# A float32 transformer stack on one core: first slots with input in five pieces, products of ones ahead of it, the first squares on GpSimd and the first mean in the third slot

## The reference

```python
def rmsnorm(x, g):
    xf = x.astype(jnp.float32)
    y = xf * lax.rsqrt(jnp.mean(xf * xf, axis=-1, keepdims=True) + EPS)
    return (y * g.astype(jnp.float32)).astype(x.dtype)

def swiglu(x, w_gate, w_up, w_down):
    return (jax.nn.silu(x @ w_gate) * (x @ w_up)) @ w_down
...
h = h + 0.5 * swiglu(rmsnorm(h, ffn1_norm[l]), ffn1_w_gate[l], ffn1_w_up[l], ffn1_w_down[l])
```

## Time and profile before

| | us |
|---|---|
| median of three runs | 1508.74 (1508.28 to 1511.12) |
| the profiled execution, its own time | 1506.61 |
| its span, first to last instruction | 1504.6 |
| TensorE busy | 1490.0 |
| VectorE busy | 1188.2 |
| ScalarE busy | 795.2 |
| GpSimd busy | 44.5 |

### The profile page before, as it was taken

The page is one execution under the profiler, slowest core; times in us unless marked ns, Lnnn a source line. Parts: engine busy times, 40 slices in busy tenths (PEclk is TensorE's granted clock), DMA queues, the critical chain, the costliest instruction groups (busy, mean ns, idle before and its releaser), DMA issues.

```text
span 1504.6 us, 25373 instructions
## 1 busy us (share of the span) xinstructions
PE 1490.0 (99%) x10802; PEld 1383.0 (92%) x10802; DVE 1188.2 (79%) x1567; ACT 795.2 (53%) x1010; POOL 44.5 (3%) x43
## 2 busy tenths in 40 slices
PE   7999999999999999999999999999999999999999
PEld 6888899999988888888899999999999999999989
DVE  7987777797898865988668678888998899766744
ACT  6444456565554443544446466455535645775653
POOL 0000001210000000000001110000000000000000
PEclk9999999999999999999999999999999999999999
DMA  7555445434555545455544443455554453325531
GB/s 284 200 194 194 172 161 188 150 141 144 191 183 192 196 172 204 184 196 195 183 164 160 180 151 141 159 223 188 200 188 180 158 195 137 117 105 190 184 125 57
DMA packets 38687, 260.50 MB, mean 173 GB/s; under 512 B 4656, under 2 KB 5040, under 8 KB 9136
## 3 DMA queue, kind: packets, MB, share of 16 engines
q1 hardware_dynamic: 37856, 257.84, 47.4%
q10 hardware_dynamic: 720, 1.05, 0.2%
HBM read 257.83 MB, written 1.05 MB: 172 GB/s over the span
## 4 chain that ended last, share of the span: by engine, by line
PE 93%; DVE 5%; ACT 1%; issue 0%; DMA 0%; ACTq 0%
PE ps L260 22%; PE ps L209 14%; PE ps L211 13%; PE ps L210 13%; PE ps L262 11%; PE ps L681 8%; PE ps L683 4%; DVE w_low L199 2%; PE ps L1400 1%; PE ps L1391 0%; PE ps L1380 0%; ACT w_high L192 0%; DMA w_raw<-in_weights 0%; DVE scratch L2072 0%; PE ps L1415 0%
## 5 line engine op out<-in xcount | busy, mean ns | idle before, releaser
L192 ACT ACTIVATE w_high<-w_raw 128x2048 fp32r<-128x2048 f32 (+3 forms) x244 | 458.5, 1880 | 407.8 <-PE ps L211 182.3
L199 DVE TENSOR_TENSOR w_low<-w_raw,w_high 128x2048 fp32r<-128x2048 f32 (+3 forms) x244 | 551.1, 2261 | 116.3 <-ACT w_high L192 114.1
L260 PE MATMUL ps<-x,w_high 128*128 128x512 f32 x1408 | 494.9, 396 | 9.4 <-DVE w_low L811 9.4
L262 PE MATMUL ps<-x,w_low 128*128 128x256 f32 x1408 | 393.6, 280 | 0.0
L260 PEld LDWEIGHTS ps<-x,w_high 128*128 128x128 f32 x1408 | 265.3, 188 | 70.9 <-issue 9.3
L262 PEld LDWEIGHTS ps<-x,w_low 128*128 128x128 f32 x1408 | 266.6, 189 | 0.1
L209 PE MATMUL ps<-x,w_high 128*128 128x256 f32 (+1 forms) x904 | 260.9, 289 | 0.5 <-DVE x L296 0.2
L211 PE MATMUL ps<-x,w_low 128*128 128x256 f32 (+1 forms) x904 | 255.7, 283 | 0.0
L210 PE MATMUL ps<-x,w_high 128*128 128x256 f32 (+1 forms) x904 | 255.6, 283 | 0.0
L681 PE MATMUL ps<-ffn_hid,w_high 128*128 128x512 f32 x528 | 183.2, 390 | 0.0
L209 PEld LDWEIGHTS ps<-x,w_high 128*128 128x128 f32 (+1 forms) x904 | 172.6, 191 | 5.5 <-issue 4.6
(11 more groups left out here) (451 smaller groups left out, 2370.0 us busy)
## 6 DMA issues: line engine op xcount, KB each, us to landing
w_raw<-in_weights SPq DMA_DIRECT2D x229, 1024.0 KB, 4.8
w_raw<-in_weights SPq DMA_DIRECT2D x10, 768.0 KB, 4.2
w_raw<-in_weights SPq DMA_DIRECT2D x5, 512.0 KB, 3.8
even_second_vectors<-in_second SPq DMA_DIRECT2D x1, 1836.0 KB, 8.2
w_raw<-in_weights SPq DMA_DIRECT2D x2, 640.0 KB, 3.9
resid<-in_x SPq DMA_DIRECT2D x4, 256.0 KB, 6.1
w_raw<-in_weights ACTq DMA_DIRECT2D x4, 256.0 KB, 7.6
out<-resid SPq DMA_DIRECT2D x3, 256.0 KB, 2.4
```

What stands on the lines that cost most here:

```text
L192: act.activation(self.wh[:, j, 0:SIZES[n]], self.raw[:, j, 0:SIZES[n]], ACT.Copy).then_inc(self.hi_made, 1)
L199: dve.tensor_tensor(self.wl[:, j, 0:SIZES[n]], self.raw[:, j, 0:SIZES[n]], self.wh[:, j, 0:SIZES[n]].bitcast(F32), ALU.subtract).then_inc( ...
L260: pe.matmul(c.bank(bank + i).rearrange("p (a t) -> p a t", a=2), wh[:, k, f], c.x[:, :, k, :], start=(k == 0), stop=False, skip_group_chec ...
L262: mm = pe.matmul(c.bank(bank + i, SEQ), wl[:, k, f], c.xh[:, k, :], start=False, stop=(k == DT - 1), skip_group_check=True)
```

## The change

- x and slot 0 arrive in five pieces: k tiles 0, 1, 2 to 3, 4 to 5, 6 to 7. The gain vector counts into the first piece's semaphore.
- TensorE issues 18 products of ones (128 x 128) as soon as the ones are there, into a bank that nothing reads.
- GpSimd squares x, two k tiles at a time, as the pieces land, and adds the squares up; ScalarE's four squares and VectorE's four additions of the first norm are gone.
- The first mean is made in the middle of slot 2, no longer in the middle of slot 1.
- In step 0 of the first stage VectorE reads the up result and makes slot 4's low part before the reciprocal, and not behind it; ScalarE makes slot 4's high part before the root.

```diff
-PIECES = 4
+FIRST_TILES = ((0, 1), (1, 2), (2, 4), (4, 6), (6, 8))
+PIECES = len(FIRST_TILES)
+WARM = 18
...
         for s in range(FF_STEPS):
+            late = s == 0 and base == 0
             dve.wait_ge(*self.filled(2 * s + 1))
             take_wide(c, dve, b.gate[:, :, :], B_GATE).then_inc(b.gate_read, 1)
             if s == 0:
                 c.split_low(dve, base + RING)
+            if late:
+                take_up(s)
+                c.split_low(dve, base + 1 + RING)
+            if s == 0:
                 self.norm.reciprocal(dve)
...
-            c.split_low(dve, base + 2 * s + 1 + RING)
+            if not late:
+                c.split_low(dve, base + 2 * s + 1 + RING)
...
-        sp.wait_ge(*self.arrived(1))
+        for b, (first, end) in enumerate(FIRST_TILES):
+            sp.dma_start(c.h[:, first:end, :], self.x[:, first:end, :]).then_inc(self.piece_in[b], 16)
+        sp.wait_ge(*self.arrived(2))
...
+        pool.wait_ge(*self.arrived(0))
+        for b in range(1, PIECES):
+            x = c.h[:, 2 * b - 2:2 * b, :]
+            pool.wait_ge(*self.arrived(b))
+            pool.tensor_tensor(c.sq[:, 2 * b - 2:2 * b, :], x, x, ALU.mult).then_inc(c.sq_made, 1)
+        pool.wait_ge(c.sq_made, PIECES - 1)
+        for i in (0, 4):
+            c.pool_link(pool.tensor_tensor(c.sq[:, i:i + 2, :], c.sq[:, i:i + 2, :], c.sq[:, i + 2:i + 4, :], ALU.add))
+        c.pool_link(pool.tensor_tensor(c.sq[:, 0:2, :], c.sq[:, 0:2, :], c.sq[:, 4:6, :], ALU.add))
+        pool.tensor_tensor(c.sq[:, 0, :], c.sq[:, 0, :], c.sq[:, 1, :], ALU.add).then_inc(c.sum_made, 1)
...
-        for b in range(PIECES):
-            self.norm.square(act, b)
         c.split_high(act, 2)
+
+    def tensor_first(self, pe):
+        c = self.c
+        pe.wait_ge(self.ones_made, 1)
+        for _ in range(WARM):
+            pe.matmul(c.bank(B_DOWN, P), c.ones[:, 0, :], c.ones[:, 1, :], start=True, stop=True)
...
-        self.norm.add(dve)
         c.split_low(dve, 2)
```

More of the change, by code:

```diff
@@ L251, in wide @@
             midway()
-        if norm and k % 2 == 0:
+        if norm and n and k % 2 == 0:
             pe.wait_ge(*norm.x_low(k // 2 + 1))
-        if n == 0 and k % 2 == 0:
-            pe.wait_ge(c.lo_made, k // 2 + 1)
+        for b, (first, _) in enumerate(FIRST_TILES if n == 0 else ()):
+            if k == first:
+                pe.wait_ge(c.xl_made, b + 1)
+                pe.wait_ge(c.lo_made, b + 1)
         if n == 1 and k % 4 == 0:
@@ L664, in tensor @@
                 pe.wait_ge(*self.gate_read(s))
-            wide(c, pe, B_GATE, base + 2 * s, norm=None if s else self.norm).then_inc(c.done, 1)
+            mean = lambda: self.norm.mean(pe)
+            wide(c, pe, B_GATE, base + 2 * s, norm=None if s else self.norm,
+                 midway=mean if s == 1 and base == 0 else None).then_inc(c.done, 1)
             if s:
                 pe.wait_ge(*self.up_read(s))
-            wide(c, pe, B_UP, base + 2 * s + 1, midway=None if s else lambda: self.norm.mean(pe)).then_inc(c.done, 1)
+            wide(c, pe, B_UP, base + 2 * s + 1, midway=mean if s == 0 and base else None).then_inc(c.done, 1)
         for m in range(FF_STEPS):
@@ L751, in __init__, with high, low @@
         self.piece_in = [c.sem(f"piece_in{b}") for b in range(PIECES)]
-        self.gain_in, self.half_in, self.tables_in, self.angle_made, self.sines_made, self.ones_made = (
-            c.sem(s) for s in ("gain_in", "half_in", "tables_in", "angle_made", "sines_made", "ones_made"))
+        self.half_in, self.tables_in, self.angle_made, self.sines_made, self.ones_made = (
+            c.sem(s) for s in ("half_in", "tables_in", "angle_made", "sines_made", "ones_made"))
     def arrived(self, b):
-        return self.piece_in[b], 32
+        return self.piece_in[b], 32 if b else 48
     def piece(self, t, b):
-        return t[:, 0, b * SLOT // PIECES:(b + 1) * SLOT // PIECES]
+        first, end = FIRST_TILES[b]
+        return t[:, 0, first * FC:end * FC]
+    def high(self, act, b):
+        c = self.c
+        act.wait_ge(*self.arrived(b))
+        for k in range(*FIRST_TILES[b]):
+            ins = act.activation(c.xh[:, k, :], c.h[:, k, :], ACT.Copy, scale=self.norm.gain[:, k:k + 1])
+        ins.then_inc(c.xh_made, 1)
+    def low(self, dve, b):
+        c = self.c
+        dve.wait_ge(c.xh_made, b + 1)
+        for k in range(*FIRST_TILES[b]):
+            ins = dve.scalar_tensor_tensor(out=c.xl[:, k, :], in0=c.h[:, k, :], scalar=self.norm.gain[:, k:k + 1],
+                                           in1=c.xh[:, k, :].bitcast(F32), op0=ALU.mult, op1=ALU.subtract)
+        ins.then_inc(c.xl_made, 1)
     def half(self, t, b):
@@ L785, in gpsimd @@
         pool.memset(c.eps[:, :], EPS).then_inc(self.ones_made, 1)
+        pool.wait_ge(*self.arrived(0))
[8 more added lines that the diff above has]
+        pool.tensor_tensor(c.sq[:, 0, :], c.sq[:, 0, :], c.sq[:, 1, :], ALU.add).then_inc(c.sum_made, 1)
     def first_scalar(self, act):
         c = self.c
[L789 to L792, removed]
+        act.dma_start(c.vec[:, 0:DT], self.vectors[:, 0:DT]).then_inc(self.piece_in[0], 16)
+        for b, (first, end) in enumerate(FIRST_TILES):
+            act.dma_start(self.piece(c.raw, b), c.weights[0][:, first * FC:end * FC]).then_inc(self.piece_in[b], 16)
         act.preload_act_table(ACT.Sqrt)
         act.wait_ge(self.ones_made, 1)
-        act.wait_ge(self.gain_in, 16)
         for b in range(PIECES):
-            self.norm.high(act, b)
+            self.high(act, b)
             act.activation(self.piece(c.wh, b), self.piece(c.raw, b), ACT.Copy).then_inc(c.hi_made, 1)
```

27 lines of the change are left out of this document (16 added, 11 removed).

## The result

| | before | changed |
|---|---|---|
| median, us | 1508.91 (1508.28 to 1511.50, 8 runs) | 1513.45 (1511.26 to 1516.82, 8 runs) |
| the profiled execution, its own time | 1506.61 | 1511.26 |
| its span | 1504.6 | 1509.2 |

The ratio is 1.0034, with an interval of 1.0024 to 1.0044: slower by 4.5 us in the medians (0.34% by the ratio), more than the 0.2% that the prediction took as the least a measurement can tell from no change, and just above the upper end of its range (1513.4). The forecast was 1511.3. The direction and the place were right, the size was not.

A forecast was written before the change was run, and what follows sets the result against it. TensorE was busy 1490 of 1504.6 us; slot 4's start was the yardstick. GpSimd's turns put it at 37.7, 2.6 us after 35.09, so 1508.74 + 2.6 = 1511.3 us; the range took in 1506.4 to 1513.4.

The forecast's parts named there:

- Who bounds the start: At slot 4's start on TensorE: VectorE's second gate read is only 0.25 us ahead and bounds it.
- Products of ones cost nothing, and their gain is not handed on: Slot 0: ones cost nothing, gain at most 2.9 us; VectorE still holds slot 4 at 35.07, TensorE waiting some 2 us.
- VectorE's new order at no cost: Step 0: uncovered copy adds 0.67 us, slot 3's low part starts at 23.08, not 23.57; slot 4 at 35.07 against 35.09.
- 10.72 us: VectorE, start of slot 3's low part to start of second gate read: 10.05 us before, 10.72 with the uncovered copy.
- GpSimd takes turns, six of them in the way: Slot 0: GpSimd and VectorE alternate by whole instructions; six GpSimd turns delay VectorE's last low part by 4.84 us.
- The terms: Added delays on the paths to slot 4: TensorE's gives 37.5, VectorE's 37.7, the later 2.6 us after 35.09.
- 5 x 0.88 + 0.44 = 4.84: Slot 0 on VectorE: five turns of 512 columns and one of 256, moving the last low part from 14.06 to 18.90.
- I leave ScalarE's start on k tiles 2 and 3 at 8.83: Slot 0: with five pieces, ScalarE was taken to begin k tiles 2 and 3 at 8.83, unchanged.
- the 11.94 from slot 3's high part to the end of the read: VectorE: 11.94 us to the second gate read's end, added to 25.65, the end of slot 3's high part; slot 4 at 37.7.
- The sum for TensorE's path: TensorE: slot 0 done at 20.44, then slots of 5.55, 5.98 (with the mean) and 5.55 us; slot 4 at 37.5.
- The bounds of the turns: Slot 4's delay: 1.9 us with 0.75 a turn, up to 4.8 with 1.17 or a landing after 7.0.
- rival A: TensorE's clock falls back in slot 0's waits; slot 4 +3.9 to +5.2 us, about 1513.2; chance 0.22.

The follow-up runs named there:

- squares back: Changed kernel with the four squares on ScalarE and the additions on VectorE again; 1510.63 us against 1511.09 before, ratio 1.0005.
- order alone: Kernel before with only the mean in slot 2 and the new order of VectorE and ScalarE in step 0; 1511.04 us, ratio 1.0002.
- gate first: Squares and additions off GpSimd, second gate read in the copy's gap, first gate read ahead of slot 2's low part and additions; 1510.38 us, ratio 0.9997.
- two more squares: Changed kernel with two more GpSimd squares of 512 columns between squares and additions; 1517.06 us (one execution), kernel before 1510.50.
- ones alone: Kernel before with only the 18 products of ones ahead; 1510.44 us against 1510.64, ratio 0.9998.
- no ones: Changed kernel without the 18 products of ones; 1513.72 us against 1510.63 for the kernel before, ratio 1.0023.
- changed, again: Changed kernel, nothing edited, measured once more on another chip; 1515.20 us against 1510.50 for the kernel before, ratio 1.0029.
- GpSimd alone: Kernel before with only the squares and additions of the first norm moved to GpSimd; 1514.34 us against 1510.63, ratio 1.0023.
- read first: Changed kernel with squares and additions off GpSimd, second gate result read while ScalarE copies the product; 1509.83 us against 1510.50 before, ratio 1.0000.
- GpSimd late: Changed kernel with GpSimd held until the low parts of slots 0 and 1 are made; 1519.35 us against 1510.50 for the kernel before, ratio 1.0062.

## Why the prediction missed

Point by point, by its own steps:

- *Who bounds the start.* Right for the changed kernel, if narrowly, and not a rule for its relatives. In five kernels (changed, squares back, order alone, gate first, two more squares) TensorE waited for VectorE's second gate read, and slot 4 began within 0.1 us of its end. In the six others TensorE came later on its own path: by 0.3 to 0.4 us in "ones alone" and "no ones", by 0.7 and 2.2 in "changed, again" and "GpSimd alone" (low clock), by 1.0 in "read first" (the first gate read) and by 3.4 in "GpSimd late" (the sum of the squares).
- *Products of ones cost nothing, and their gain is not handed on.* Right in the time, 0.9998 [0.9989, 1.0007]. Of the kernels with the ones and an undisturbed VectorE, the mechanism named, VectorE holding slot 4, is seen only in "squares back" and "gate first", where TensorE waited 0.3 and 0.6 us for it, not some 2; in "ones alone" the gain went at the mean.
- *VectorE's new order at no cost.* Right in the time, 1.0002 [0.9993, 1.0011], and its 10.72 us were met. That it costs nothing at slot 4 needed an earlier start of slot 3's low part; where that start stayed at 23.55 ("squares back"), slot 4 was 0.45 later.
- *GpSimd takes turns, six of them in the way.* Right in mechanism and in number: "GpSimd alone" and "squares back" turn the loss on and off, and the lengthened rows are those named.
- *The terms.* This is the step that failed: the sum made slot 4 2.6 us late, and it was 3.81. "5 x 0.88 + 0.44 = 4.84" measured 5.6 where the pieces came as before ("GpSimd alone"), and 5.2 in the changed kernel, where "I leave ScalarE's start on k tiles 2 and 3 at 8.83" was 9.24: either way slot 0's last low part ends at 19.67 and not at 18.90, 0.8 later. A turn amid work of both engines was 0.78 to 1.18 us, where one row of 0.88 had been taken for all. And the 11.94 from slot 3's high part to the end of the read had no wait in it; in the changed kernel slot 4's load landed after 6.3 us, and VectorE waited 0.37 for its high part. The forecast's 2.6 with 0.8 and 0.4 is the 3.8 measured at slot 4. The sum for TensorE's path was short too, 37.5 against 38.70: besides the later low part, it took 5.55 us for a slot, where the earlier trace rows have 5.62 and 5.66 from start to start and the changed kernel took 5.65 for slot 1 and 5.71 for slot 3. The bounds of the turns (1.9 to 4.8) held the 3.8, and the 4.5 of the medians; the range ended at the middle of rival A instead.
- *Rival A as an alternative.* This failed in kind. I priced a lower clock as another way for the change to go, with a chance of 0.22. It comes on top of the turns in some executions and not in others of the same kernel: slot 4 at 39.92 and 40.00 in two of the four traces with GpSimd's squares in slot 0 and the turns of the changed kernel, 38.90 and 38.97 in the other two. A median over executions holds a share of it. The 4.5 us of the medians are 0.7 more than the 3.8 at slot 4. Such a share would account for them, and so would the stretches of slower pace in the last section; no run parts the two, and that 0.7 us stays open. So does what decides the moment at which the clock rises.

## What to carry to other kernels

Work moved to GpSimd is not free for VectorE, even if GpSimd is 96% idle: where VectorE's instructions have two inputs in SBUF, count about the length of GpSimd's own instruction (0.78 to 1.18 us a turn, where a square alone took 1.04) for each that falls into a stretch in which VectorE is the bound. Beside VectorE's reads of PSUM no such price was seen. And the other way round: the result of work on GpSimd beside a full VectorE comes later by VectorE's instruction at each turn, so it must not be one that others wait for. An earlier start is worth only what the next binding engine hands on; in "ones alone" 2.4 us at slot 1 became 0.6 at slot 4 and nothing in the medians.

When a mechanism can act in some executions alone, add its price times its share to each case, instead of setting it beside them as a rival.

## What the runs showed that I had not expected

**Stretches at a slower pace with the clock granted in full.** Of the 4.65 us between the profiled executions 0.8 come behind slot 4. In the kernel before, the pairs of a slot stand 0.347 us apart nearly everywhere, as here (TensorE's timeline, 12 pairs, 4.16 us):

```profile
640.16 0.39 PE L260 MATMUL ps<-x,w_high 128*128 128x512 f32 x1
...
644.32 0.39 PE L260 MATMUL ps<-x,w_high 128*128 128x512 f32 x1
...
1017.56 0.40 PE L260 MATMUL ps<-x,w_high 128*128 128x512 f32 x1
...
1021.80 0.40 PE L260 MATMUL ps<-x,w_high 128*128 128x512 f32 x1
```

From 1017.56, though, 12 pairs took 4.24 us, 0.353 each, at a granted clock of 1.00. Such a stretch lasts 110 to 160 us and costs about 2 us; that of the kernel before goes from 1004 to 1162. The changed kernel has one at another place: by the times of the same up reads in both, the difference was 3.9 us up to 624, grew from 4.4 at 634 to 6.2 at 723, fell from 6.1 to 4.7 between 1018 and 1182, where the kernel before had its stretch, and was 4.6 at the end. In all twelve traces they stand at the same few places (from about 20 to 140, 420 to 545, 615 to 730 and 1010 to 1160), and an execution has between one and three of them, some only in part: "changed, again" has three, and the two before 550 alone add 4.2 us to its distance from the kernel before. What makes them stays open. One is about a quarter of the spread of the kernel before over all sessions (1505.4 to 1513.8), so two profiled executions are to be compared station by station.

**The turns are whole instructions, from both sides.** That GpSimd gets its turn between back-to-back instructions was in the earlier trace rows. That it waits itself, up to 2.3 us at a time, behind VectorE's long ones was expected for "GpSimd late", but not how late its sum would be: 32.5 us, and the experiment that was to rescue the idea became the slowest kernel. The Trainium skill's "GPSIMD Engine Reference", section "Specifications", says that the two share SBUF interfaces; the runs agree, and put 0.8 to 1.2 us on a turn of 512 columns.
